# Eleven tile transposes moved from TensorE to the DMA engines, and the projection stages reordered, in an eight-core decoder layer

## The reference, cut to what matters

```
h = rmsnorm(x)
[u | v | p | q | gate_logits] = h @ w_in
A: a = gelu(u) * (tril(W_s[g]) @ LN(gelu(v)) + b_s[g])   per chunk of 128 positions, 4 groups
B: b = scale * groupwise_linear(mean over trailing 2,4,8,16 of p  -  p)
C: 4-head attention of q into 256 memory rows; K, V = rmsnorm(mem) @ w_kv
x += (sig(g_A)*P_A(a) + sig(g_B)*P_B(b) + sig(g_C)*P_C(c)) @ w_o
x += relu(rmsnorm(x) @ w_up)^2 @ w_down
y = rmsnorm(x)
```

## Time and profile before

| | us |
|---|---|
| median of 3 runs | 944.57 |
| lowest, highest | 944.48, 945.01 |
| the profiled execution | 943.52 |
| its span on the slowest core (7) | 942.0 |
| spans of all cores | 938.8 to 942.0 |
| PE, DVE, ACT, POOL busy in that span | 909.1, 387.8, 303.5, 281.6 |

### The profile page before, as it was taken

One profiled execution on the slowest core, in us unless ns is written; L12 is line 12 of the kernel. 1 busy time (PEld: TensorE's weight loads), 2 busy tenths in 40 slices (PEclk: granted clock), 3 DMA queues, 4 the chain that ended last, 5 costly groups with the idle time before them and its releaser, 6 DMA issues.

```text
span 942.0 us, 15396 instructions; the slowest of 8 cores (938.8 to 942.0 us)
## 1 busy us (share of the span) xinstructions
PE 909.1 (97%) x5187; PEld 464.5 (49%) x5187; DVE 387.8 (41%) x642; ACT 303.5 (32%) x532; POOL 281.6 (30%) x289
## 2 busy tenths in 40 slices
PE   6899989999999999999999999999999999999995
PEld 2555545444555555544455444554445544455442
DVE  3667755224322222247532343223432244322576
ACT  3346755874222222223333001330013300133232
POOL 3243316233433333334333101331013310133243
PEclk9989999999999999999999999999999999999998
DMA  8973468105672210278640503105031050310134
GB/s 181 237 187 96 91 113 139 48 6 85 189 126 46 46 31 16 45 216 153 102 79 1 90 1 59 32 1 90 1 57 34 1 90 1 60 31 1 68 148 165
DMA packets 34634, 74.39 MB, mean 79 GB/s; under 512 B 19950, under 2 KB 20973, under 8 KB 31102
## 3 DMA queue, kind: packets, MB, share of 16 engines
q0 software_dynamic: 7344, 40.90, 24.3%
q1 hardware_dynamic: 27068, 32.48, 12.0%
q10 hardware_dynamic: 146, 0.04, 0.0%
HBM read 94.49 MB, written 10.22 MB: 111 GB/s over the span
## 4 chain that ended last, share of the span: by engine, by line
PE 89%; DMA 5%; ACT 1%; issue 1%; DVE 1%; POOL 0%; DVEq 0%; SPq 0%; POOLq 0%; ACTq 0%
PE bank L352 88%; DMA X<-bsx 2%; DMA slot<-wpk 2%; DMA CR<-ck 1%; PE bank L355 1%; ACT L358 1%; ACT X L358 0%; DVE X L370 0%; DVE hT L376 0%; DVEq L128 0%; ACT fA L358 0%; ACT CR L358 0%; POOL stats L361 0%; DVE stats L589 0%; POOL X L159 0%
## 5 line engine op out<-in xcount | busy, mean ns | idle before, releaser
L352 PE MATMUL bank<-hT,slot 128*128 128x436 bf16 (+3 forms) x2480 | 466.5, 347 | 4.2 <-DVE hT L376 2.0
L352 PEld LDWEIGHTS bank<-hT,slot 128*128 128x128 bf16 x2480 | 239.0, 98 | 217.7 <-issue 8.3
L352 PE MATMUL bank<-slot,CR 128*128 128x512 bf16 (+1 forms) x1376 | 296.3, 378 | 0.0
L358 ACT ACTIVATE fA<-bank 128x436 f32<-128x436 f32 (+2 forms) x215 | 115.6, 545 | 340.0 <-PE bank L352 319.6
L352 PEld LDWEIGHTS bank<-slot,CR 128*128 128x128 bf16 x1376 | 134.6, 98 | 160.5
L370 DVE SCALAR_TENSOR_TENSOR X<-bank,stats,X 128x512 f32<-128x512 f32 x136 | 102.0, 750 | 119.8 <-PE bank L352 119.8
L358 ACT ACTIVATE fW<-bank 128x436 f32<-128x436 f32 (+2 forms) x103 | 54.8, 535 | 164.1 <-PE bank L352 162.4
L361 POOL TENSOR_TENSOR CR<-fA 128x436 bf16<-128x436 f32 (+1 forms) x69 | 67.5, 980 | 108.9 <-ACT fA L358 105.0
L361 DVE TENSOR_TENSOR CR<-fA 128x436 bf16<-128x436 f32 (+1 forms) x51 | 32.8, 646 | 116.8 <-ACT fA L358 116.8
L361 DVE TENSOR_TENSOR fA<-bank,fA 128x436 f32<-128x436 f32 (+1 forms) x77 | 42.9, 605 | 78.6 <-PE bank L352 75.2
L361 POOL TENSOR_TENSOR stats<-stats,nhalf 128x1 f32<-128x1 f32 (+3 forms) x34 | 37.7, 1110 | 107.0 <-DVE stats L367 65.6
(11 more groups left out here) (95 smaller groups left out, 475.0 us busy)
## 6 DMA issues: line engine op xcount, KB each, us to landing
slot<-wpk POOLq DMA_DIRECT2D x27, 1024.0 KB, 12.3
X<-x SPq DMA_DIRECT2D x24, 512.0 KB, 9.8
y<-hT SPq DMA_DIRECT2D x17, 512.0 KB, 2.7
X<-x POOLq DMA_DIRECT2D x10, 512.0 KB, 9.5
slot<-wpk POOLq DMA_DIRECT2D x6, 512.0 KB, 18.1
CR<-ck POOLq DMA_DIRECT2D x4, 512.0 KB, 10.0
CR<-cv POOLq DMA_DIRECT2D x4, 512.0 KB, 12.4
CR<-mem SPq DMA_DIRECT2D x2, 512.0 KB, 24.5
```

Source lines behind the costliest of these rows:

```text
L352: s.op("pe", lambda e: e.matmul(out, lhsT=lhsT, rhs=rhs, start=start, stop=stop), R_, W_)
L358: s.op("act", lambda e: e.activation(out=out, in_=in_, func=func, **kw), R_, W_)
```

## The change

- Tiles 8 to 16 and the memory rows (100, 101) are no longer transposed by `T` or `trans`. `dma_trans` issues one DMA on SP that transposes the scaled bf16 rows into `hT` or `hmT`. For tiles from 8 on, `N(t)` issues it itself.
- The scaling of these rows is called earlier. For tiles 8 to 11 the squares stand between the projections of block 1, and `N(8)` and `N(9)` ahead of `WIN(1)`.
- In block 1 the four `U` come first and the four `MIX` after them. Tile 2's transpose goes ahead of the first half of tile 1's v projection, and tile 3's copy moves from ACT to DVE.
- `setup_loads` waits for the load of tile 5 (`xst_b[1]`) in place of a weight half, and `mem_loads` for the load of tile 7 (`xst_b[3]`).
- In block 2, `S(0, 0)`, the four `vout` and `WIN(2)` are called twice, and `S(0, 1)` comes after them. `U(2, 0)` stands ahead of `AV(0, 0)`.
- The load of tile 16 and its squares are called within block 2, ahead of `P(12)`. `Q(3)` stands ahead of `P(15)`, and `P(14)` ahead of `Q(3)`.
- In the gate stage the sample groups 2 and 3 (`SA1` to `SA3`) are called one step later.

```diff
-            s.dma("sp", [(gm, gvec[1].partition_broadcast(128))], writes=gm_b, owner=mem_o)
+            s.dma("sp", [(gm, gvec[1].partition_broadcast(128))], writes=gm_b, owner=mem_o, after=[xst_b[3]])
+        def dma_trans(t, dst, dst_bufs, col0):
+            xn, xnb = xn_of.pop(t)[0:2]
+            s.dma("sp", [(dst[:, :, col0:col0 + 128], xn, True)], reads=[xnb], writes=dst_bufs, owner=dst_bufs[0])
         def N(t):
             norm_c(t, gb[:], gb_b)
+            if t >= 8:
+                dma_trans(t, hT, [hT_b[t]], t * 128)
...
-        setup_loads([slot_b[1][0]])
+        setup_loads([xst_b[1]])
...
+        N(8)
+        N(9)
         WIN(1)
+        N(10)
         us = [U(1, 0)]
-        N(nx[0])
-        us.append(U(1, 1))
-        MIX(1, 0, *us[0])
...
+        N(11)
+        for g in range(1, 4):
+            us.append(U(1, g))
+        load_x(BT[3])
+        mst = norm_a([100, 101])
+        for g in range(4):
+            MIX(1, g, *us[g])
+        norm_b(*mst)
...
         S(0, 0)
-        S(0, 1)
+        for i in range(4):
+            vout(i)
+        N(14)
+        WIN(2)
+        S(0, 0)
         for i in range(4):
             vout(i)
         WIN(2)
+        S(0, 1)
+        us = [U(2, 0, True)]
         AV(0, 0)
-        T(nx[0])
-        us = [U(2, 0, True)]
...
-        N(nx[2])
+        N(15)
+        load_x([16])
...
-        load_x([16])
+        n16 = norm_a([16])
         MIX(2, 3, *us[3])
+        norm_b(*n16)
...
-        T(15)
         S(1, 0)
+        N(16)
+        P(14)
         Q(3)
         S(1, 1)
-        n16 = norm_a([16])
-        norm_b(*n16)
-        P(14)
         P(15)
```

More of the change, by code:

```diff
@@ L905, in build_program @@
         vpart(0, 0)
+        T(2, "act")
         vpart(1, 0)
-        T(2, "act")
+        T(3)
         vpart(2, 0)
-        T(3, "act")
         vpart(3, 0)
@@ L931, in build_program @@
             us.append(U(0, g, parts=(1,)))
-            na.append(norm_a([4 + g]))
+            if g:
+                na.append(norm_a([3 + g]))
+        na.append(norm_a([7]))
         setup_ops(0)
@@ L955, in build_program @@
         P(5)
-        load_x(BT[2], queue="pool")
-        load_next("kv")
         mem_loads()
@@ L961, in build_program @@
         hst = hist_loads()
+        load_x(BT[2], queue="pool")
+        load_next("kv")
+        nx = BT[2]
+        na = norm_new(4)
         vmm(2)
         P(6)
+        norm_sq(na, 8)
+        norm_sq(na, 9)
         vmm(3)
         P(7)
-        Q(1)
-        nx = BT[2]
-        na = norm_a(nx)
+        norm_sq(na, 10)
+        norm_sq(na, 11)
+        Q(1)
         vfin()
@@ L974, in build_program @@
             vout(i)
+        N(8)
+        N(9)
         WIN(1)
+        N(10)
         us = [U(1, 0)]
-        N(nx[0])
-        us.append(U(1, 1))
-        MIX(1, 0, *us[0])
[L980 to L983, removed]
+        N(11)
+        for g in range(1, 4):
+            us.append(U(1, g))
+        load_x(BT[3])
         mst = norm_a([100, 101])
+        for g in range(4):
+            MIX(1, g, *us[g])
         norm_b(*mst)
-        N(nx[2])
[L987 to L992, removed]
         nx = BT[3]
         P(8)
-        T(10, "act")
         P(9)
-        T(11, "act")
         norm_c(100, gm, gm_b)
+        dma_trans(100, hmT, hmT_b, 0)
         P(10)
@@ L1003, in build_program @@
         norm_c(101, gm, gm_b)
+        dma_trans(101, hmT, hmT_b, 128)
         P(11)
-        trans(100, hmT, hmT_b, 0, "act")
         na = norm_a(nx[0:2])
@@ L1008, in build_program @@
         vmm(0)
-        trans(101, hmT, hmT_b, 128, "act")
         norm_b(*na)
@@ L1013, in build_program @@
         nb = norm_a(nx[2:4])
-        N(nx[0])
+        N(12)
         norm_b(*nb)
@@ L1019, in build_program @@
         vmm(3)
-        N(nx[1])
+        N(13)
         vfin()
         S(0, 0)
-        S(0, 1)
+        for i in range(4):
[3 more added lines that the diff above has]
+        S(0, 0)
         for i in range(4):
@@ L1033, in build_program @@
         us.append(U(2, 1))
-        N(nx[2])
+        N(15)
+        load_x([16])
         MIX(2, 0, *us[0])
         us.append(U(2, 2))
-        T(nx[1], "act")
         MIX(2, 1, *us[1])
-        N(nx[3])
         us.append(U(2, 3))
-        T(nx[2], "act")
         MIX(2, 2, *us[2])
-        load_x([16])
+        n16 = norm_a([16])
         MIX(2, 3, *us[3])
+        norm_b(*n16)
         kvs_load(0)
@@ L1060, in build_program @@
         AV(1, 1)
-        N(16)
         s.dma("sp", [(gb[:], gbv.partition_broadcast(128))], writes=[gb_b], owner=gb_b)
@@ L1067, in build_program @@
         vmm(1)
-        T(16)
         vmm(2)
+        vmm(3)
         Q(4)
-        vmm(3)
         P(16)
@@ L1160, in build_program @@
             (2, 2): lambda: (SA3(0), SA3(1)),
[L1161 to L1164, removed]
+            (1, 3): lambda: (SA1(2), SA1(3)),
+            (2, 3): lambda: (SA2(2), SA2(3)),
+            (0, 4): lambda: (SA2b(2), SA2b(3)),
         }
@@ L1181, in build_program @@
                 G(1, 4)
+                SA3(2)
+                SA3(3)
             B(m, si)
```

## The result

The changed kernel takes 957.75 us (median of four executions; three of them at 955.11 to 957.97) against 944.79 (944.48 to 945.27) for the kernel before on the same chip: a ratio of 1.0126, interval 1.0106 to 1.0145. It is slower, as forecast, but by 12 to 13 us where I had 3. That is the upper end of my range of 936 to 957: the median lies 0.75 above it, while the ratio, put on the 944.57 that I started from, gives 956.5.

The account below looks back on a forecast made before the run. PE was taken as the bound, with 89% of the chain of waits. Terms -2.4 + 3.8 - 0.1 - 1.2 = +0.1, plus 2.9 for the clock, gave +3.0 on 943.52; with 1.05 for the median, 947.6 us, range 936 to 957.

Parts of the forecast that it names:

- Work, -3.1: PE's work: eleven tile transposes leave, -5.0 us; the second `S(0, 0)` and `WIN(2)` add 0.45 and 1.4.
- Start, -0.8: Start of the kernel: DVE's 0.76 us wait for tile 7's statistics goes, taken as -0.8, bounds -3 to +3.
- rival 2: Setup transfers land late behind tile 5, PE waits 13 us more before the first `MIX`: 960.6 us, chance 0.08.
- `KV`, wait 2.3: Block 1: `KV` waits 2.3 us for late memory-row transposes, yet `S(0, 0)` starts 2.4 us earlier than before.
- `S(0, 1)`, +3.8 to `P(12)`: Block 2: PE waits 3.1 us at `S(0, 1)` for DVE's casts; `S(0, 0)` to `P(12)` takes 3.8 us longer.
- Block 3, -0.1: `P(12)` to `WIN(3)`: new waits at `Q(3)` and `S(1, 1)` cancel removed transposes and their waits, 24.8 us against 24.9.
- my signs of being wrong: Signs against the forecast: `WIN(3)` before 138, a wait at the first `MIX`, transposes landing after over 6 us.
- Rival 3: Transposes land late behind the loads of tiles 12 to 15, so `KV` comes 13 us later: 960 us, chance 0.07.
- Later, -1.2: Gate stage: sample scores come one step later, so the 1.16 us wait at `ck` goes, -1.2 us.
- Clock, one fall, +2.9: Three idle spells on PE bring one fall to half clock, costing 2.9 us; ends were none and three, +8.7.

Follow-up runs that it names:

- c4: c1's order with all transposes on TensorE and no gate on the sample cache loads: 958.2 us, ratio 1.001 to the kernel before.
- c1: b3 together with c3, and `N(14)` moved behind `WIN(2)`: 949.5 us, ratio 0.991 to the kernel before.
- a1: The changed kernel with `S(0, 0)`, the four `vout` and `WIN(2)` called once: 953.32 us, ratio 1.0078 to the kernel before.
- b1: The changed kernel with the setup transfers waiting again for the weight half, as in the kernel before: 967.1 us, ratio 1.013 on cores 0 to 3.
- b2: The changed kernel with the memory tiles' `norm_b` after block 1's first `MIX`, not all four: 962.1 and 961.3 us, ratio 1.013 on cores 0 to 3.
- c3: The changed kernel with memory tile 101's transpose freed of waiting for tile 100's landing: 964.7 us, ratio 1.010 on cores 0 to 3.
- a2: The changed kernel with the sample cache loads (`kvs_load`) issued behind the load of `mrg3`: 951.91 us, ratio 1.0061 to the kernel before.
- a3: The changed kernel with tile 16's load moved from behind `N(15)` to behind `load_next("mrg0")`: 956.01 us, ratio 1.0108 to the kernel before.
- a4: The changed kernel with filler matmuls, 8 before `KV`, 12 before `S(0, 1)`, 12 before `Q(4)`: 955.02 us, ratio 1.0094 to the kernel before.
- c2: The changed kernel's order, doubled calls included, with transposes on TensorE: 964.9 us, ratio 1.007 on cores 0 to 3.
- b3: The changed kernel with a1, a3, b1, b2 and the cache loads gated behind tile 16's transpose: 955.5 us, ratio 0.995 to the kernel before.

## Why the prediction was right in sign and short in size

- **Work, -3.1:** nothing speaks against it, but no run measures it alone. c4 against c1 gives 6.4 to 8.7 for the -5.0 together with the waits at copies; a1 gives the +1.9 together with a wait.
- **Start, -0.8:** about right on the fast cores, wrong on core 5. `WIN(0)` started 0.1 to 1.3 us earlier than before on cores 1, 2, 4 and 6, and 0.3 to 2.6 later on the four others. On core 5 rival 2 came true in part: `bsx` landed 9.3 us after its issue at 36.4 (20.2 in the earlier trace rows), DVE waited 2.98 for it, and `T(5)` came at 50.08, 1.8 later than on core 7 before; on cores 1, 2 and 4 `bsx` landed after 4.4 to 4.7. It is not the 13 us of rival 2, and b1 shows no gain from undoing it.
- **`KV`, wait 2.3:** 2.68 on core 5, 1.12 to 3.40 over the cores. The size was near by luck, since the reason was wrong in part: I had the power behind POOL's products and then each transpose at 2.9, and did not see that the second waits for the first to land. b2 moved the power and the wait stayed; c3 freed the second transpose and it went to 0.96.
- **`S(0, 1)`, +3.8 to `P(12)`:** right in kind and size: 2.91 us behind the cast (3.1 forecast) on five cores, on the others partly in the stop within `WIN(2)`, which I did not foresee. That stop stands in the traces of the changed kernel, a2, a3, b1, b2 and c3, always after 19 matmuls, and in a4 after 11; it stands in none of the kernels that call `WIN(2)` once, nor in c2. What ends it stays open. `P(12)` came 22.0 after `S(0, 0)`, where I had 18.9: the clock fell in `U(2, 0)`.
- **Block 3, -0.1:** ACT waited for tile 16 as forecast (3.52 against 3.3), and `Q(3)` 0.92 (1.0), but `S(1, 1)` did not wait (3.6 forecast). Instead the step failed at a place that it did not name: I let tile 16's transpose land after 2.9, while `kvs_load` puts 2 MB ahead of it. The landing took 14.9, and PE waited 3.50 at `Q(4)`. Landings of over 6 us were among my signs of being wrong. The Trainium skill's page "DMA: Bandwidth & Descriptors" says in the section "Queues, rings and completion order" that an engine alternates between its queues by packets. I took that to mean that a small transfer on SP passes POOL's loads, and here it did not. In packets the transpose is not small: from 128 to 150 us on core 5 the loads' queue moved 576 packets (2.10 MB), and there were 1151 packets of under 512 bytes, most of them on the other queue. By alternation nearly all of the loads would then go ahead of the transpose's last packet, which fits the 14.9; this is argued from the counts, and no run tests it. I had counted the loads of x tiles as the transposes' neighbours, and not the loads that POOL issues. Rival 3 had the mechanism, at the wrong tile.
- **Later, -1.2:** the wait at `ck` is gone, but PE waits 1.30 at 259.24 behind a cast. `SA3` now stands at another place there, which I take for the cause; no run tests it. Nothing is gained on core 7, and cores 1, 3, 5 and 6, which had no wait of over 0.5 at `ck` before, lose 1.0 to 1.4.
- **Clock, one fall, +2.9:** this is the term that was mis-sized most. A fall costs 1.6 to 3 us; cores 1, 2, 4 and 6 had one after 60 us, core 0 two, cores 3, 5 and 7 three (6.3 on core 5). I took the likely number for one core. The time is that of the slowest of eight, and some core had two or three falls in each of the four executions, going by its span.

Cores 1, 2, 4 and 6 fit the sum, as a number: they start `WIN(3)` at 140.9 to 142.1, 2.2 to 3.4 us later than before, where the forecast was 141 to 145. Part of that is luck, since the sum lacks the wait at `Q(4)` and has one at `S(1, 1)` that did not come. On the other four it is the second and third fall and the longer waits at `KV` and `Q(4)`.

What stays open is why some cores fall at a wait that others pass. The length of the wait explains the profiled execution of the changed kernel, but not all runs: in c2 all eight cores wait the same 2.29 us at `P(8)` and five of them fall, and in b3 core 0 passes 3.20 at `KV` where core 2 falls at 2.98. In a4, with fillers ahead of it, a wait of 2.90 brought none.

## What to carry to other kernels

A transpose moved from TensorE to DMA turns 0.45 us of work plus a copy into a latency of 3 us, and into 13 to 17 where bulk loads of another queue are issued ahead. It pays once each tile is scaled a stage ahead, bulk loads are gated behind the transposes, and two transposes into one tensor don't wait for each other in the schedule's book. For a program on eight cores, price each new wait of some 2.3 us or more by the wait and a half-clock stretch behind it, and do it for the unluckiest core, not for the mean one.

## What the runs showed of the hardware

- The transpose of one tile (128 x 1024, bf16) landed 3.0 to 3.1 us after its issue with nothing ahead, 3.1 to 8.0 with the loads of tiles 12 to 15 issued some 2 to 6 us before, and 13.0 to 15.6 in the changed kernel with four loads of 512 KB issued by another engine's queue in the 2 us before (12.7 to 16.9 in a3).
- In the changed kernel waits of PE of 2.31 to 4.14 us were followed by a clock near 0.50 for up to 6 us (110 to 116 on core 5), at one to three places by core; waits of 2.26 and less were not, nor were those of 1.45 in the kernel before. Other runs have exceptions between 2.0 and 3.2 us.
- By the ratio to the kernel before, single repairs gave 4.5 us (a1), 6.1 (a2), 1.7 (a3) and 3.0 (a4), and c3 3.8 by the slowest of cores 0 to 3; b1 and b2 gave nothing clear. All of them but the fillers together, with the cache loads gated in place of a2's later ones and with `N(14)` moved (c1), gave 20.4 by the ratio and 19.6 on those cores, a little more than the sum of the single ones.
